# The first three value units taken by halves: first halves of all three, then second halves

## The reference

```python
h = rms_norm(x, norm_pre_g)
proj = einsum('bsd,de->bse', h, w_in)
q_a, k_a, v_a, g_a, f_a, q_b, k_b, v_b, g_b = split(proj)   # 512 columns each, f_a 8
log_f = log_sigmoid(f_a + fox_forget_b)
y_a = fox_attention(q_a, k_a, v_a, log_f) * silu(g_a)       # 8 heads of 64, causal, forget bias
y_b = moba_attention(q_b, k_b, v_b, slopes) * silu(g_b)     # 8 heads of 64, ALiBi, one block here
y = concat(y_a, y_b) @ w_out
out = x + rms_norm(y, norm_post_g)
```

## Time and profile before

| | |
|---|---|
| median of 3 runs | 147.05 us (146.78 to 147.18) |
| the profiled execution | 147.58 us, span 145.8 us |
| PE busy | 137.5 us, 94% of the span |
| DVE busy | 110.8 us, 76% |
| ACT busy | 99.6 us, 68% |
| transfers | 26.96 MB, mean 185 GB/s, up to 406 GB/s in a fortieth of the span |

### The profile page before, as it was taken

The page is one execution under the profiler, slowest core; times in us unless marked ns, Lnnn a source line. Parts: engine busy times, 40 slices in busy tenths (PEclk is TensorE's granted clock), DMA queues, the critical chain, the costliest instruction groups (busy, mean ns, idle before and its releaser), DMA issues.

```text
span 145.8 us, 2904 instructions
## 1 busy us (share of the span) xinstructions
PE 137.5 (94%) x1076; PEld 129.0 (88%) x1076; DVE 110.8 (76%) x243; ACT 99.6 (68%) x209; POOL 44.7 (31%) x70
## 2 busy tenths in 40 slices
PE   7999999999999999999999999999999999999920
PEld 7899899999999999998899999999999888898910
DVE  0384965999999996679989898989899866240891
ACT  4466989488957488598568788795959495244530
POOL 2621100000000012019293755465472924200241
PEclk9999999999999999999999999999999999999996
DMA  4899997488876999941744443525174000000034
GB/s 90 268 323 396 400 389 296 127 334 241 288 214 216 323 378 406 368 161 18 270 148 144 146 144 103 189 66 216 27 246 173 0 0 4 0 0 0 0 144 144
DMA packets 9725, 26.96 MB, mean 185 GB/s; under 512 B 1384, under 2 KB 2416, under 8 KB 9456
## 3 DMA queue, kind: packets, MB, share of 16 engines
q1 hardware_dynamic: 9120, 25.57, 50.7%
q10 hardware_dynamic: 592, 1.22, 2.5%
HBM read 25.73 MB, written 1.06 MB: 184 GB/s over the span
## 4 chain that ended last, share of the span: by engine, by line
PE 43%; DVE 24%; DMA 15%; ACT 6%; issue 4%; SPq 3%; POOL 2%; POOLq 1%; ACTq 0%; DVEq 0%
PE bank L850 20%; PE bank L1011 13%; DVE w_lo L570 11%; DMA h<-in_x 6%; DMA raw_out<-in_w_out 5%; DMA raw<-in_w_units 4%; PE bank L944 4%; DVE h L614 2%; DVE v L628 2%; DVE gate L635 2%; SPq L207 2%; DVE h_lo L641 2%; DVE wo_lo L646 2%; PE bank L961 1%; ACT w_hi L369 1%
## 5 line engine op out<-in xcount | busy, mean ns | idle before, releaser
L570 DVE TENSOR_TENSOR w_lo<-raw,w_hi 128x1024 fp32r<-128x1024 f32 (+1 forms) x33 | 44.2, 1343 | 8.4 <-ACT w_hi L369 8.4
L369 ACT ACTIVATE w_hi<-raw 128x1024 fp32r<-128x1024 f32 (+1 forms) x33 | 34.5, 1057 | 6.4 <-DMA raw<-in_w_units 4.6
L850 PE MATMUL bank<-h_hi,w_hi 128*128 128x256 f32 x128 | 36.7, 286 | 0.0
L850 PE MATMUL bank<-h_hi,w_lo 128*128 128x256 f32 x128 | 35.6, 278 | 0.0
L850 PE MATMUL bank<-h_lo,w_hi 128*128 128x256 f32 x128 | 35.6, 278 | 0.0
L850 PEld LDWEIGHTS bank<-h_hi,w_hi 128*128 128x128 f32 x128 | 24.1, 188 | 0.9
L850 PEld LDWEIGHTS bank<-h_hi,w_lo 128*128 128x128 f32 x128 | 24.0, 188 | 0.0
L850 PEld LDWEIGHTS bank<-h_lo,w_hi 128*128 128x128 f32 x128 | 24.0, 188 | 0.0
L324 POOL TENSOR_TENSOR probs<-probs,row_inv 128x256 f32<-128x256 f32 (+1 forms) x16 | 12.9, 828 | 23.0 <-DVE row_inv L715 23.0
L850 PE MATMUL bank<-xg_hi,w_hi 128*128 128x256 f32 x64 | 17.9, 280 | 0.0
L310 POOL TENSOR_TENSOR bias<-squares,causal 128x256 f32<-128x256 f32 x4 | 6.2, 1548 | 37.7 <-DMA squares<-decay_rows_scratch 37.7
(11 more groups left out here) (131 smaller groups left out, 318.5 us busy)
## 6 DMA issues: line engine op xcount, KB each, us to landing
raw<-in_w_units SPq DMA_DIRECT2D x30, 512.0 KB, 5.4
raw_out<-in_w_out SPq DMA_DIRECT2D x4, 512.0 KB, 6.6
raw<-in_w_out SPq DMA_DIRECT2D x4, 512.0 KB, 3.4
h<-in_x SPq DMA_DIRECT2D x2, 512.0 KB, 8.0
squares<-decay_rows_scratch ACTq DMA_DIRECT2D x1, 1024.0 KB, 7.9
x_t<-in_x SPq DMA_DIRECT2D x1, 1024.0 KB, 7.6
raw<-in_w_units SPq DMA_DIRECT2D x3, 256.0 KB, 4.8
out<-x_t SPq DMA_DIRECT2D x3, 256.0 KB, 2.0
```

Source lines behind the costliest of these rows:

```text
L369: nc.scalar.activation(w[0][:, s, 0:width], raw[:, s, 0:width], ACT.Copy).then_inc(s_hi, 1)
L570: nc.vector.tensor_tensor(w[1][:, s, 0:width], raw[:, s, 0:width], w[0][:, s, 0:width].bitcast(F32), ALU.subtract).then_inc(s_lo, 1)
L850: last = nc.tensor.matmul(dst, stationary(a, j), moving(b, j), start=n == 1, stop=n == count * len(PASSES))
```

## The change

The table of pieces becomes one list over all three units. SP, ACT, DVE and PE walk through it in this order: 0a, 0b, 1a, 2a, 0c, 1b, 2b. Unit 2 is loaded in two halves, and 0c is one piece of 520 columns instead of pieces of 256 and 264. Unit 3 and everything behind it keep their order.

```diff
-PIECES = (((0, SEQ), (SEQ, HALF), (HALF, HALF + SEQ), (HALF + SEQ, V_WIDTH)), ((0, HALF), (HALF, V_WIDTH)),
-          ((0, HALF), (HALF, V_WIDTH)))
+PIECES = ((0, 0, SEQ), (0, SEQ, HALF), (1, 0, HALF), (2, 0, HALF),
+          (0, HALF, V_WIDTH), (1, HALF, V_WIDTH), (2, HALF, V_WIDTH))
...
-            load_x(0)
-            load_values(0, 0, SEQ, s_piece_in[0])
-            load_values(0, SEQ, HALF, s_piece_in[1])
-            load_values(0, HALF, D_MODEL, s_raw_in[0])
-            load_x(1)
-            load_values(1, 0, HALF, s_piece_in[2])
-            load_values(1, HALF, D_MODEL, s_raw_in[1])
...
+            for g, (u, lo, hi) in enumerate(PIECES):
+                if lo == 0:
+                    load_x(u)
+                if hi == V_WIDTH:
+                    load_values(u, lo, D_MODEL, s_raw_in[u])
+                else:
+                    load_values(u, lo, hi, s_piece_in[g])
+            load_x(PIECED)
+            load_values(PIECED, 0, D_MODEL, s_raw_in[PIECED])
...
-            for u in range(PIECED):
-                pieced_unit(u)
+            for g, piece in enumerate(PIECES):
+                value_piece(g, *piece)
```

More of the change, by code:

```diff
@@ L40 @@
 V_GROUPS = ((0, HALF), (HALF, HALF + SEQ), (HALF + SEQ, V_WIDTH))
-PIECES = (((0, SEQ), (SEQ, HALF), (HALF, HALF + SEQ), (HALF + SEQ, V_WIDTH)), ((0, HALF), (HALF, V_WIDTH)),
-          ((0, HALF), (HALF, V_WIDTH)))
-PIECED = len(PIECES)
-PIECES_BEFORE = (0, 3, 4)
+PIECES = ((0, 0, SEQ), (0, SEQ, HALF), (1, 0, HALF), (2, 0, HALF),
+          (0, HALF, V_WIDTH), (1, HALF, V_WIDTH), (2, HALF, V_WIDTH))
+PIECED = 3
 G_UNITS, QK_UNITS = PAIRS, 2 * PAIRS
@@ L151, in hybrid_layer @@
         s_raw_in = [sem(f"raw_in{s}") for s in range(RING)]
-        s_piece_in = [sem(f"first_piece_{c}_in") for c in range(3)]
+        s_piece_in = [sem(f"first_piece_{g}_in") for g in range(len(PIECES) - PIECED)]
         s_wf_in, s_wf = sem("w_f_in"), sem("forget_columns")
@@ L208, in load_values @@
                              w_units[units, :, part][0:n].rearrange("a p c -> p a c")).then_inc(landed, 16)
-            load_x(0)
-            load_values(0, 0, SEQ, s_piece_in[0])
-            load_values(0, SEQ, HALF, s_piece_in[1])
-            load_values(0, HALF, D_MODEL, s_raw_in[0])
-            load_x(1)
-            load_values(1, 0, HALF, s_piece_in[2])
-            load_values(1, HALF, D_MODEL, s_raw_in[1])
-            for u in range(2, RING):
-                load_x(u)
-                load_values(u, 0, D_MODEL, s_raw_in[u])
+            for g, (u, lo, hi) in enumerate(PIECES):
[7 more added lines that the diff above has]
+            load_values(PIECED, 0, D_MODEL, s_raw_in[PIECED])
             def load_unit(r, s):
@@ L388, in x_high @@
                                      scale=gpre_col[:, j:j + 1]).then_inc(s_xghi, 1)
-            for c, (lo, hi) in enumerate(X_LOADS):
+            for g, (u, lo, hi) in enumerate(PIECES):
+                if lo == 0:
+                    act.wait_ge(s_x_in[u], 16)
+                    x_high(u)
+                if hi == V_WIDTH:
+                    act.wait_ge(s_raw_in[u], 16)
+                    act.wait_ge(s_wf, u + 1)
+                    nc.scalar.activation(w[0][:, u, lo:hi], raw[:, u, lo:hi], ACT.Copy).then_inc(s_hi, 1)
+                else:
+                    act.wait_ge(s_piece_in[g], 16)
+                    nc.scalar.activation(w[0][:, u, lo:hi], raw[:, u, lo:hi], ACT.Copy).then_inc(s_piece_hi, 1)
+            for c in range(PIECED, len(X_LOADS)):
                 act.wait_ge(s_x_in[c], 16)
-                for j in range(lo, hi):
+                for j in range(*X_LOADS[c]):
                     x_high(j)
[L394 to L402, removed]
+                if c < RING:
                     unit_high(c, 16, width=V_WIDTH)
@@ L579, in x_low @@
                                                op0=ALU.mult, op1=ALU.subtract).then_inc(s_xglo, 1)
-            for c, (lo, hi) in enumerate(X_LOADS):
-                for j in range(lo, hi):
-                    x_low(j)
[L584 to L591, removed]
+            for g, (u, lo, hi) in enumerate(PIECES):
+                if lo == 0:
+                    x_low(u)
+                last = hi == V_WIDTH
+                dve.wait_ge(s_hi if last else s_piece_hi, u + 1 if last else g + 1)
+                nc.vector.tensor_tensor(w[1][:, u, lo:hi], raw[:, u, lo:hi], w[0][:, u, lo:hi].bitcast(F32),
+                                        ALU.subtract).then_inc(s_lo if last else s_piece_lo, 1)
+            for c in range(PIECED, len(X_LOADS)):
+                for j in range(*X_LOADS[c]):
+                    x_low(j)
+                unit_low(c % RING, c + 1, V_WIDTH)
             unit_low(2, 7, V_WIDTH)
@@ L864, in value_part, with value_piece @@
                 return last
-            def pieced_unit(u):
+            def value_piece(g, u, lo, hi):
+                last = hi == V_WIDTH
+                done = u + 1 if last else g + 1
+                parts = [(max(lo, a), min(hi, b)) for a, b in V_GROUPS if a < hi and b > lo]
                 pe.wait_ge(s_xghi, u + 1)
[L868 to L882, removed]
+                pe.wait_ge(s_hi if last else s_piece_hi, done)
+                for a, b in parts:
+                    value_part(u, 0, a, b)
+                pe.wait_ge(s_xglo, u + 1)
+                for a, b in parts:
+                    value_part(u, 1, a, b)
+                pe.wait_ge(s_lo if last else s_piece_lo, done)
+                for a, b in parts:
+                    ins = value_part(u, 2, a, b)
+                if last:
+                    ins.then_inc(s_used, 1)
             def value_unit(u):
```

## The result

The changed kernel takes 148.62 us (median of 9 runs, 148.55 to 149.09); the kernel before took 147.18 us in the same comparison (9 runs, 146.43 to 148.12). The ratio is 1.0101, with a 95% interval of 1.007 to 1.0133: slower by about 1%, where I had forecast no change. The profiled execution took 148.62 us, its span is 146.8.

The account below looks back on a forecast made before the run. The DVE chain until 71.85 us, then PE, was taken to set the end. 0.60 at 7.44, less 0.27 at 14.66, less 0.10 at 51.73 and about half the rest: +0.1, 147.15 us, range 146.6 to 147.9.

Parts of the forecast that it names:

- The transfer queue: At 11 to 13 us: unit 4's later load arrives as the queued bytes run out, 11.8 against 11.95; no loss.
- the first of my rivals: Transfer queue runs dry at 11 to 13 us, delaying the rows of x: priced 0.8 us, 147.85 us, chance 0.12.
- longest start: Longest delay from unit 4's issue to its bytes, 2.4 us: 10.7 + 2.4 = 13.1, queue 1.15 us dry.
- From the rows of x to the end: DVE chain from the rows of x, landing at 21.41, to 71.85 has no slack; later landing moves the end one to one.
- PE's room: At 71.85 us PE could be 0.7 us later without moving the end: 0.5 there plus 0.2 waiting for POOL.
- The faster rival: Rows of x land 0.5 us earlier than 21.41, DVE chain gets earlier: -0.37 to -0.5 us, 146.6, chance 0.11.
- PE's pause at 1a: At 7.44 us PE waits for 1a's rounding until about 7.91; with a slower start, 0.60 us late.
- a sign of being wrong: In the profile after, 1a's rounding later than 7.6 or earlier than 7.0 us would show the prediction wrong.
- The stall at unit 3: Around 14.66 us PE lost 0.27 us on unit 3's high part; the change was to remove this.
- The figure from the Trainium skill: Fixed cost of about 2.0 us per transfer; taken all as start delay of unit 4's load, 0.75 us more.
- The clock rival: PE's pause at 7.44 us puts its clock back to 1.2 GHz: some 1.2 us reach the end, 148.3, chance 0.03.

Follow-up runs that it names:

- the first experiment: Kernel before, only SP's wait ahead of unit 4's load raised from one finished unit to two: 148.42 us, ratio 1.0088.
- the changed kernel again: The changed kernel, unaltered, measured and profiled a second time, in a later set: 149.95 us, ratio 1.0204 to the kernel before.
- the larger dose: Kernel before, SP waiting for three finished units instead of one ahead of unit 4's load: 151.10 us, ratio 1.0297.
- the faster execution of before: Second profiled execution of the kernel before, unchanged: 146.75 us.
- the two pairs with own buffers: Changed kernel and kernel before, unit 4 in its own buffer: 147.37, 147.21 us; units 4 and 5 in own buffers, rows of x issued early: 147.88, 148.41 us.
- x ahead: Kernel before, unit 4's load waiting for two finished units, x for units 6 and 7 issued ahead of that wait: 147.71 us, ratio 1.0011.
- the new load order alone: Kernel before with only SP's order of first loads as in the changed kernel; ACT, DVE and PE keep the old order: 150.70 us, ratio 1.0277.
- the kernel before with the rows ahead: Kernel before, SP issuing x for units 6 and 7 and both halves of the rows of x before waiting for unit 0: 149.50 us, ratio 1.0199.

## Why the prediction was wrong

**The transfer queue was the step that failed.** "The first bytes after an issue at 0.74 appear between 1.75 and 2.00, so about 1.1 us later, and unit 4's would come at 11.8. It is a tie, and I take no loss". The place, the issue (10.32 where I had 10.5 to 10.9) and the moment at which the bytes run out (the rate falls from 12 us on, I had 11.95) were right. The price was 1.96 us at the rows of x in place of 0. The start of the program showed when the first bytes flow, not when the flow is full: there, too, the rate was about 200 GB/s and less until 4 us, as the trace of before has it:

```profile
1.00:2.00 1.00, 1.00 (x4) 1.00 (x5) 0.00 (x0) 0.81 (x1) 0.61 (x3) 1.00 0.12 33
2.00:3.00 1.00, 1.00 (x7) 1.00 (x6) 0.00 (x0) 0.67 (x2) 0.00 (x0) 1.00 0.85 202
3.00:4.00 1.00, 1.00 (x7) 1.00 (x6) 0.02 (x1) 0.51 (x1) 0.00 (x0) 1.00 0.69 137
```

A queue that has run short moves 365 GB/s or more again only 5.7, 5.8, 6.4 and 7.2 us after the first new issue (the changed kernel, the first experiment, the changed kernel again, the larger dose). It was the first of my rivals, priced at 0.8 us with a chance of 0.12, and its longest start, 2.4 us, did not reach the case.

**From the rows of x to the end.** I wrote that the DVE chain "has no slack", and that the end follows that landing one to one when it is later. That held. In the first experiment PE's broadcast products after unit 6 start at 25.96, in the faster execution of before at 26.03, so PE itself is not late; the squares of the first norm give their sum 1.34 us later, and the last stretch of products starts at 128.56 instead of 127.24, 1.32 us later:

```profile
128.56 7.04 PE bank L1011 x42
```

```profile
127.24 7.04 PE bank L1011 x42
```

In the changed kernel it starts at 129.13, 1.89 later than the second of these. Three waits make it up, read against the same execution of before (17.57 for unit 4, 26.39 for unit 7, 37.53 for gate unit 11):

```profile
17.99 1.18 PE L862 MATMUL bank<-w_hi,xg_hi 128*128 128x512 f32 x6 [0.18 <-ACT w_hi L367]
...
27.50 1.18 PE L862 MATMUL bank<-w_hi,xg_hi 128*128 128x512 f32 x6 [0.24 <-ACT w_hi L367]
...
39.46 0.39 PE L852 MATMUL bank<-xg_hi,w_hi 128*128 128x256 f32 x1 [0.41 <-DVE gate L637]
```

0.42 us late at unit 4, whose load landed at 16.7; 1.11 at unit 7, whose rounding ACT does only after `rstd`'s root and a table load; 1.93 at gate unit 11, which waits for DVE's second gate product, at the tail of the shifted DVE row. After it PE does not wait again. The difference of the medians, 1.44 us, is smaller than 1.89; the runs of before scatter over 1.7 us and those of the changed kernel over 0.5.

**PE's room was misread, though the loss does not hang on it.** "At 71.85 PE has 0.7 us of room" was true of the profiled execution, which at 147.58 us was in the upper half of the runs of before, and not of every execution. I had noted the distance to the median and not asked what it consisted of. With the two profiles of each kernel the loss can be read both ways. Without these waits the last stretch moves from 127.24 to 129.13, by 1.89. With them it moves from 128.10 to 130.37, by 2.27, for rows of x that land 2.14 later. It comes through in both. The faster rival lived on the waits alone, and has nothing to win in an execution without them.

**PE's pause at 1a** was right in kind. 1a was rounded from 6.88 on, where I had 7.26 and had called anything before 7.0 a sign of being wrong; PE went on at 7.66 and not at 7.91, after a wait:

```profile
7.66 0.70 PE L862 MATMUL bank<-w_hi,xg_hi 128*128 128x512 f32 x2 [0.35 <-ACT w_hi L398]
```

By 14.81, the start of unit 3, PE was 0.08 us behind the 14.73 of the faster execution of before, which itself paused 0.7 us for 0c. The pause costs nothing that shows, and the two pairs with own buffers agree (147.37 and 147.21 us; 147.88 and 148.41). The stall at unit 3 is not there (its first pass takes 0.93 us, from 14.81 to 15.74), as forecast, but that is luck: the faster execution of before has none either (0.95, from 14.73 to 15.68). Unit 4 had a new one.

**The figure from the Trainium skill.** I had set the fixed cost of about 2.0 us, in the Trainium skill, DMA: Bandwidth & Descriptors, section "Anatomy of one DMA", aside because bytes flowed 1.1 us after an issue. That section gives the figure for transfers that POOL issues, which I had not said; these are SP's. Taken as a delay it would have given +0.75 us, an estimate, with the right sign and too small. No run here shows a cost per transfer as the reason, since in the full queue hundreds of kilobytes pass at 400 GB/s behind the same issues.

**What stays open:** why the flow takes so long to recover while loads stand issued, with engines in part idle and in part slow, and why the rate rises and then falls a second time (clearly in the larger dose and in the changed kernel again, faintly with x ahead). That the late issue makes the dip and the late rows of x is shown; how the transfer system makes it that long is not. Open too is what makes the `raw_out` load late in some executions.

## What to carry to other kernels

A load into a ring slot waits for the unit that holds the slot, so an order that finishes unit 0 late moves not one load but all that SP has queued behind it; count for each new order when each slot comes free, and where that load's bytes stood in the queue. Where a queue is near its end, take the refill as several microseconds, from a stretch in which it did refill, and not from the first byte of the first load. And before giving a delay "room" at a later wait, profile the kernel a second time: a wait that only some executions have is no room to count on.

## What the runs showed of the hardware

A transfer queue that has run short can recover in steps. In the larger dose, after an issue at 12.82, it moved 281 and 305 GB/s at 14 to 16 us, then 41 and 123 at 16 to 18, and 352 only from 19 on, with five more loads issued by 15.57. In the second run of the changed kernel, after an issue at 11.63, it moved 326 GB/s at 13 to 14 us, 76 at 15 to 16, and 377 only from 18 on.

The clock rival did not come, but a longer pause shows what it would have been. In the run with the new load order alone PE stood idle for 2.76 us, up to 9.81, and its granted clock (fourth column) was at the 1.2 GHz level from 9.5 to about 12.8 us. All the shorter pauses in the other traces, up to the 2.19 us ahead of 20.05 in the kernel before with the rows ahead, left it at 2.4 GHz:

```profile
8.00:9.00 1.00, 0.00 (x0) 1.00 0.99 299
9.00:10.00 1.00, 0.18 (x1) 0.75 0.97 348
10.00:11.00 1.00, 1.00 (x5) 0.50 1.07 406
11.00:12.00 1.00, 1.00 (x7) 0.50 1.00 381
12.00:13.00 1.00, 1.00 (x6) 0.55 0.80 285
13.00:14.00 1.00, 1.00 (x6) 1.00 0.92 297
```
